# The modulation product of block 1's mixers: fp32 weights against split halves with four stationary columns

## The chip, the cores and the metric

The kernel runs on one core of a Trainium2 chip. The metric is device time in microseconds (us) of one execution. The median of three executions of the kernel before is 5227.35 us (5226.25 to 5237.21). The engines are named as in the profile: PE is the matrix engine (PEld its weight loads), DVE the vector engine, ACT the scalar engine, SP the engine that issues the transfers of the weights.

## The reference, cut to what matters

The model is two blocks. Block 1 has attention beside a state-space mixer and a feed-forward layer. Block 2 is modulated: two conditioning vectors of 2048 numbers go through SiLU and one matrix, and the six parts of the result shift, scale and gate the block's activations.

```python
# block 2, one layer; c_ctx serves the context, c the tokens
mod_c = jax.nn.silu(c_ctx) @ w_ada[l][:, :n_mod * D_MODEL] + b_ada[l][:n_mod * D_MODEL]
mod   = jax.nn.silu(c)     @ w_ada[l] + b_ada[l]          # 2048 -> 6 * 2048
sh1, sc1, g1, sh2, sc2, g2 = [m[:, None, :] for m in jnp.split(mod, 6, axis=-1)]
y, _ = _token_mixers(_modulate(x, sh1, sc1), lp, ctx_states, True, True)
```

`w_ada` is 2048 x 12288 in fp32, 100 MB. Nothing in it depends on block 1, so the kernel computes the product while block 1's mixers run.

## The kernel before, in words

All weights stream through one ring of 8 slots of 128x512 fp32 (`weights_ring`). SP issues the transfer of a chunk (256 KB) when the chunk 8 places ahead of it is marked `ring_free`. A group is 512 output columns. A group of `w_ada` is 16 chunks, one per 128 of the 2048 inputs, and there are 24 groups, so 384 chunks.

Most products are split (`split_scalar`, `split_vector`, `split_tensor`): for every chunk ACT copies the weights into the type fp32r (`weights_hi`, L511), DVE subtracts that from the chunk (`weights_lo`, L526), and PE multiplies low weights by high activations, high by low and high by high (L547 to L549). There are 5 pairs of halves in rotation. `w_ada` is not split before the change: `modulation_tensor` multiplies the fp32 chunk as the moving operand (512 columns) against two stationary columns, the two vectors (`cc`, L1088). That takes nothing from ACT or DVE but, once a group, ACT's copy of the 2x512 result (L1101) and its store.

The stage around the change is `mixers1`. It has 4 turns. In a turn, two strands run in lockstep: attention (8 units of a head and a query tile, 6 pieces each) and two channel blocks of the state-space mixer (16 pieces each). `beside` gives, after every piece of the strands, as many steps of the background as keep pace with 56 pieces; the background is six groups of `w_ada` of 17 steps, of which 16 are chunks. So each piece is followed by 102/56 = 1.82 steps, that is 1.71 chunks, and the strands end after 49 pieces; the steps left over run by themselves at the turn's end. The three engines write out their instructions in this same order, each for its own part. The order of an engine is the order of its code, and one semaphore counts each engine's finished instructions, so nothing is reordered at run time.

The pieces of a channel block, by number, on DVE: 1 masks and copies (L1025, L1026, L625); 2 the phases (L1034); 3 L1037; 4 L1040, then ACT's sine (L1073), L1042, then ACT's cosine (L1075); 5 empty; 6 to 13 the eight inner steps j; 14 L1057; 15 L1059; 16 L1061; and L1065 at the start of the next block, behind PE's sixteen products L1013 and L1014. An inner step is: PE multiplies twice (L1006, L1007), DVE forms the rotated input (L1049, L1050, L1052) and scans it (L1054). PE's next pair waits for L1050 (`turned`). A unit of attention is PE L863, DVE L892, L895, L897, ACT L923 and L924 (exponential), DVE L900, L902, L904, PE L870, DVE L908 and L909, PE L876, DVE L625.

Of the kernel before, what the change touches and what calls it, by code (L numbers as in the profile page):

```python
# [6 lines left out]
F32 = mybir.dt.float32  # L7
# [237 lines left out]
class Kernel:  # L245
# [4 lines left out]
    def __init__(self, nc, io, known, pofs, cofs):  # L250
        self.nc, self.io, self.pofs, self.cofs = nc, io, pofs, cofs
        self.s = Signals(nc, known)
        self.s.sem("vector_done")
        sb = lambda name, *shape, dt=F32: nc.alloc_sbuf_tensor(name, [P, *shape], dt)
        self.ring = sb("weights_ring", self.SLOTS, self.COLS)
        self.whi, self.wlo = (sb(n, self.HALVES, self.COLS, dt=F32R) for n in ("weights_hi", "weights_lo"))
        self.acc = [nc.alloc_psum_tensor(f"acc{m}", [P, 512], F32) for m in range(4)]
        self.bank = [nc.alloc_psum_tensor(f"bank{b}", [P, 512], F32) for b in range(4)]
        self.params = sb("params_sb", max(b for a, b in pofs.values()))
        self.consts = sb("consts_sb", max(b for a, b in cofs.values()))  # L260
        self.res = sb("residual", KD, L)

        with nc.sbuf_tensor("moving_halves", [P, KD, 512], F32R) as self.xin_r:
            pass
        self.xin = sb("moving", KD, 512)
        self.mix = sb("mixed", 16, T)
        self.rstd = sb("rstd", L)
        self.mods = sb("mods", 96, 2)
        self.cc, self.cc_sig = sb("cc", 32), sb("cc_sig", 32)
        self.mods_row = sb("mods_row", 512)  # L270
        self.ab = sb("ab", 4, 32)
        self.whole = sb("whole_i32", 64, dt=I32)[:, :]
        with nc.sbuf_tensor("arena_halves", [P, ARENA], F32R) as self.arena_r:
# [97 lines left out]
    def plan(self):  # L371
# [30 lines left out]
        for n in range(5):  # L402
            add("w_in", n, io["w_in"], n, KD, L, keep_projection, **x1)
        for n in range(24):
            add("w_ada", n, io["w_ada"], n, KD, 0, None)
        for n in range(2):
            add("w_glu", n, io["w_glu"], n, 8, T, keep_gate, **moving(T))
        for n in range(4):
# [24 lines left out]
        for g in order:  # L433
            g.ring0, g.split0 = ring, split
            ring += g.kchunks
            split += g.kchunks if g.split else 0
            side = g.index % 2 if g.split else 0
            banks = [0] if g.name == "w_ada" else range(4 * side, 4 * side + 4) if g.tokens > T else range(2 * side, 2 * side + 2)
            if g.name == "read" and g.split:
                banks = [0, 1] if side else [4, 5]  # L440
            at = [(self.acc + self.bank)[b] for b in banks]
            if g.name == "w_ada":
                g.out = [at[0][0:2, :]]
            elif g.tokens > T:
                g.out = [at[m][:, 0:g.tokens] for m in range(4)]
            else:
                g.out = [at[m // 2][:, T * (m % 2):T * (m % 2 + 1)] for m in range(4)]
            g.shared = 0 < g.tokens <= T
            g.before = sorted({holder[b] for b in banks if b in holder})
            for b in banks:  # L450
                holder[b] = (g.name, g.index)
# [316 lines left out]
def project1_scalar(k):  # L768
# [3 lines left out]
    a.dma_start(k.res[:, :, :], io["hT"].rearrange("(c p) t -> p c t", p=P)).then_inc(*s.landed("inputs", "inputs"))  # L772
    a.wait_ge(*s.at("inputs"))
    a.activation(k.cc_sig[:, :], k.p("c"), ACT.Sigmoid).then_inc(*s.made("scalar_done", "cc_sig"))
    squares_scalar(k, "rms1", k.res[:, :, :], k.squares1, L)
    split_scalar(k, k.some("w_in", *range(5)), {0: operand_scalar("w_in", lambda kc: k.squares1[:, kc, :])})
    barrier(k, "scalar", "project1")
# [7 lines left out]
def project1_vector(k):  # L785
    v, s = k.nc.vector, k.s
    v.wait_ge(*s.at("inputs"))
    v.wait_ge(*s.at("cc_sig"))
    v.tensor_tensor(k.cc[:, :], k.p("c"), k.cc_sig[:, :], ALU.mult).then_inc(*s.made("vector_done", "cc"))
    root_vector(k, "rms1", KD, L)  # L790
    make = lambda k, c: normalise(k, k.res[:, :, :], k.p("norm_mix_g"), k.squares1, c, L)
    split_vector(k, k.some("w_in", *range(5)), {0: operand_vector("w_in", lambda kc: k.squares1[:, kc, :], make)})
    barrier(k, "vector", "project1")
# [285 lines left out]


def modulation_tensor(k, g):
    pe, s = k.nc.tensor, k.s
    ccv = k.cc[:, :].rearrange("p (c m) -> p c m", m=2)
    for name, index in g.before:
        pe.wait_ge(*s.at("drained", name, index))
    for kc in range(g.kchunks):
        pe.wait_ge(*s.at("weights", g.ring0 + kc))
        mm = pe.matmul(g.out[0], ccv[:, kc, :], k.slot(g.ring0 + kc), start=kc == 0, stop=kc == g.kchunks - 1)  # L1088
        mm.then_inc(*s.made("tensor_done", "ring_free", g.ring0 + kc))
        yield  # L1090
    s.mark("tensor_done", "summed", g.name, g.index)
    yield

def modulation_scalar(k, g):
    a, s = k.nc.scalar, k.s
    for _ in range(17):
        yield
    a.wait_ge(*s.at("summed", g.name, g.index))
    if g.index:
        a.wait_ge(*s.at("mods_out", g.index - 1))  # L1100
    a.activation(k.mods_row[0:2, :], g.out[0], ACT.Copy).then_inc(*s.made("scalar_done", "drained", g.name, g.index))  # L1101
    a.wait_ge(*s.now("scalar_done"))
    a.dma_start(k.io["s_mods"][:, 512 * g.index:512 * g.index + 512], k.mods_row[0:2, :]).then_inc(
        *s.landed("mods_out", "mods_out", g.index))

def modulation_vector(k, g):
    for _ in range(17):
        yield

def pair_of(channels, k, turn):  # L1110
    yield from channels(k, 2 * turn)
# [7 lines left out]
def mixers1_tensor(k):  # L1119
    heads_tensor(k)  # L1120
    barrier(k, "tensor", "heads")
    k.nc.tensor.wait_ge(*k.s.at("cc"))
    mixers1(k, attention_tensor, channels_tensor, modulation_tensor)
    barrier(k, "tensor", "mixers1")

# [16 lines left out]
def output1_scalar(k):  # L1142
# [13 lines left out]
    split_scalar(k, k.feed_forward("w_up", "w_down"), {0: operand_scalar("w_up", lambda kc: k.mix[:, kc, :])})  # L1156
    barrier(k, "scalar", "w_down")
    a.wait_ge(*s.at("mods_out", 23))
    rows = k.mix[0:96, 0:2, 0:P]
    for r in range(2):  # L1160
        a.dma_start(rows[:, r, :], k.io["s_mods"][r:r + 1, :].rearrange("a (c p) -> (a c) p", p=P)).then_inc(*s.landed("mods_in"))
    s.mark("mods_in", "mods_in")

def output1_tensor(k):
# [7 lines left out]
    squares_tensor(k, "rms2", k.mix, KD, T)  # L1172
    split_tensor(k, k.feed_forward("w_up", "w_down"))
    barrier(k, "tensor", "w_down")
    rows = k.mix[0:96, 0:2, 0:P]
    pe.wait_ge(*s.at("mods_in"))
    for r in range(2):
        pe.transpose(k.bank[r][:, 0:96], rows[:, r, :], k.ident[0:96, 0:96]).then_inc(*s.made("tensor_done", "mods_t", r))

def output1_vector(k):  # L1180
# [23 lines left out]
    for r in range(2):  # L1204
        v.wait_ge(*s.at("mods_t", r))
        serial(k, v.tensor_tensor(k.mods[:, :, r], k.bank[r][:, 0:96], k.p("b_ada"), ALU.add))
    for c in (16, 64):
        serial(k, v.tensor_scalar(k.mods[:, c:c + 16, :], k.mods[:, c:c + 16, :], 1.0, None, ALU.add, ALU.bypass))

# [1072 lines left out]
```

## Time and profile before

| | us |
|---|---|
| median of three executions | 5227.35 |
| the profiled execution | 5236.34 |
| its span, first to last instruction | 5234.9 |
| PE busy in the span | 4389.1 |
| DVE busy | 2903.7 |
| ACT busy | 1562.3 |

Busy time says how long an engine had something running; a wait inside a stage shows in the views of that stage. The program runs stage by stage with barriers between. The stage of the mixers lies between about 195 us, where PE's first product of the modulation starts, and 870 us. Times in the rows below are us from the start of the span unless they are marked ns. "x4" after a row is the count of records in it. A product of fp32 by fp32 is recorded twice, so the 384 products of L1088 are 768 records.

### The profile page before, as it was taken

What the parts mean: (1) busy time and instruction counts of PE and PEld (TensorE: products, weight loads), DVE (VectorE), ACT (ScalarE), POOL (GpSimd) and SP (SyncE); (2) the same over time, 40 slices, a digit from 0 to 9 for tenths busy, and PEclk for the clock granted to TensorE, in tenths of its full rate; (3) what the DMA queues carried; (4) which work ended last, traced back from release to release, by engine and by line L of the source; (5) the groups of instructions that cost most, each with busy time, mean ns of one, the idle gap of its engine ahead of it and who ended that gap; (6) DMA issues with size and microseconds to landing.
All of it is one profiled execution on the core that took longest, in us unless ns stands there. A gap on an engine that the chain in (4) does not pass through costs nothing.

```text
span 5234.9 us, 70641 instructions
## 1 busy us (share of the span) xinstructions
PE 4389.1 (84%) x28352; PEld 3731.8 (71%) x28352; DVE 2903.7 (55%) x6102; ACT 1562.3 (30%) x2706; POOL 0.2 (0%) x4
## 2 busy tenths in 40 slices
PE   7588887899999899993478876788775798999997
PEld 7323323799999888892467766677662397999997
DVE  4745544575565522345665666656626475755654
ACT  4211111454444322342122121221200043544442
POOL 0000000000000000000000000000000000000000
PEclk9799998999999999995689988899896799999999
DMA  5354454465656544571222222222240163555553
GB/s 176 97 171 141 141 163 147 129 186 185 184 186 183 158 121 122 144 198 45 60 69 81 61 64 71 68 83 61 62 129 22 39 208 128 178 189 184 184 185 113
DMA packets 383061, 669.57 MB, mean 128 GB/s; under 512 B 43897, under 2 KB 77402, under 8 KB 382220
## 3 DMA queue, kind: packets, MB, share of 16 engines
q1 hardware_dynamic: 327168, 595.74, 38.0%
q10 hardware_dynamic: 55564, 69.31, 4.0%
q8 instruction: 223, 3.65, 0.3%
q14 instruction: 106, 0.87, 0.1%
HBM read 634.87 MB, written 29.46 MB: 127 GB/s over the span
## 4 chain that ended last, share of the span: by engine, by line
PE 64%; DVE 13%; ACT 2%; issue 2%; DMA 1%; ACTq 1%; DVEq 0%
PE acc L547 13%; PE acc L549 12%; PE acc L548 12%; PE acc L589 8%; PE bank L1611 2%; PE bank L547 2%; PE bank L549 2%; PE bank L548 2%; PE bank L1620 2%; PE bank L1618 1%; PE bank L2005 1%; DVE arena L1466 1%; DMA arena<-s_read 1%; ACT weights_hi L511 1%; PE acc L1435 1%
## 5 line engine op out<-in xcount | busy, mean ns | idle before, releaser
L526 DVE TENSOR_TENSOR weights_lo<-weights_ring,weights_hi 128x512 fp32r<-128x512 f32 x1600 | 1093.9, 691 | 1042.5 <-ACT weights_hi L511 1041.1
L511 ACT ACTIVATE weights_hi<-weights_ring 128x512 fp32r<-128x512 f32 x1600 | 992.9, 629 | 1102.6 <-PE acc L549 905.3
L548 PE MATMUL acc<-arena_halves,weights_hi 128*128 128x256 f32 (+2 forms) x3136 | 925.3, 295 | 0.0
L547 PE MATMUL acc<-arena_halves,weights_lo 128*128 128x256 f32 (+1 forms) x2944 | 870.0, 296 | 18.2 <-DVE weights_lo L526 17.9
L549 PE MATMUL acc<-arena_halves,weights_hi 128*128 128x256 f32 (+1 forms) x2944 | 869.1, 295 | 0.0
L547 PE MATMUL acc<-moving_halves,weights_lo 128*128 128x256 f32 (+1 forms) x2816 | 795.7, 283 | 69.8 <-DVE weights_lo L526 68.3
L549 PE MATMUL acc<-moving_halves,weights_hi 128*128 128x256 f32 (+1 forms) x2816 | 791.0, 281 | 0.0
L548 PE MATMUL acc<-moving_halves,weights_hi 128*128 128x256 f32 x2624 | 735.8, 280 | 0.0
L548 PEld LDWEIGHTS acc<-arena_halves,weights_hi 128*128 128x128 f32 x3136 | 602.4, 192 | 12.6
L547 PEld LDWEIGHTS acc<-moving_halves,weights_lo 128*128 128x128 f32 x2816 | 538.6, 191 | 77.7 <-DVE weights_lo L526 50.5
L547 PEld LDWEIGHTS acc<-arena_halves,weights_lo 128*128 128x128 f32 x2944 | 565.7, 192 | 31.9 <-DVE weights_lo L526 12.3
L549 PEld LDWEIGHTS acc<-arena_halves,weights_hi 128*128 128x128 f32 x2944 | 565.7, 192 | 12.9
L589 PE MATMUL acc<-moving,weights_ring 128*128 128x256 f32 x2304 | 554.3, 387 | 2.1 <-ACT arena L692 2.1
L549 PEld LDWEIGHTS acc<-moving_halves,weights_hi 128*128 128x128 f32 x2816 | 535.1, 190 | 0.0
L548 PEld LDWEIGHTS acc<-moving_halves,weights_hi 128*128 128x128 f32 x2624 | 499.7, 190 | 0.0
L589 PEld LDWEIGHTS acc<-moving,weights_ring 128*128 128x128 f32 x2304 | 428.8, 195 | 52.3 <-ACT arena L692 2.5
L1088 PE MATMUL acc<-weights_ring,cc 128*2 128x512 f32 x768 | 367.0, 614 | 12.2 <-ACT mods_row L1101 12.1
L1088 PEld LDWEIGHTS acc<-weights_ring,cc 128*2 128x2 f32 x768 | 55.2, 85 | 244.7 <-issue 219.0
L548 PE MATMUL bank<-arena_halves,weights_hi 128*128 128x256 f32 (+2 forms) x640 | 209.0, 327 | 0.0
L549 PE MATMUL bank<-arena_halves,weights_hi 128*128 128x512 f32 (+1 forms) x512 | 172.0, 336 | 0.0
L547 PE MATMUL bank<-arena_halves,weights_lo 128*128 128x512 f32 (+1 forms) x512 | 172.0, 336 | 0.0
L1739 ACT ACTIVATE arena<-bank 128x512 f32<-128x512 f32 x112 | 65.7, 594 | 298.7 <-PE bank L1611 297.1
(409 smaller groups left out, 5088.8 us busy)
## 6 DMA issues: line engine op xcount, KB each, us to landing
weights_ring<-in_w_in SPq DMA_DIRECT2D x624, 256.0 KB, 2.7
weights_ring<-in_w_ff SPq DMA_DIRECT2D x512, 256.0 KB, 3.0
weights_ring<-in_w_ada SPq DMA_DIRECT2D x384, 256.0 KB, 3.0
weights_ring<-in_w_up SPq DMA_DIRECT2D x256, 256.0 KB, 3.0
weights_ring<-in_w_down SPq DMA_DIRECT2D x256, 256.0 KB, 3.3
weights_ring<-in_w_out SPq DMA_DIRECT2D x128, 256.0 KB, 3.2
weights_ring<-in_w_branch SPq DMA_DIRECT2D x96, 256.0 KB, 3.2
s_state<-arena ACTq DMA_DIRECT2D x36, 256.0 KB, 2.9
```

Source lines behind the costliest of these rows:

```text
L511: a.activation(whi, k.slot(g.ring0 + kc), ACT.Copy).then_inc(*s.made("scalar_done", "high", n))
L526: v.tensor_tensor(wlo, k.slot(g.ring0 + kc), whi.bitcast(F32), ALU.subtract).then_inc(*s.made("vector_done", "low", n))
L547: pe.matmul(g.out[m], wlo[:, cols], xhi, start=first, stop=False, skip_group_check=g.shared)
L548: pe.matmul(g.out[m], whi[:, cols], xlo, start=False, stop=False, skip_group_check=g.shared)
L549: mm = pe.matmul(g.out[m], whi[:, cols], xhi, start=False, stop=last, skip_group_check=g.shared)
L589: mm = pe.matmul(g.out[m], k.slot(g.ring0 + kc)[:, m * P:(m + 1) * P], g.x(kc), start=kc == 0 and m % 2 == 0, stop=last, skip_group_check= ...
L1088: mm = pe.matmul(g.out[0], ccv[:, kc, :], k.slot(g.ring0 + kc), start=kc == 0, stop=kc == g.kchunks - 1)
L1435: mm = pe.matmul(po[:, P * j:P * j + P], h["lev"][:, j, :], h["lev"][:, j, :], start=True, stop=True)
L1466: own(v.reciprocal(f, f))
L1611: mm = pe.matmul(b0[:, P * j:P * j + P], mt[:, j, :], x[:, j, :], start=True, stop=True)
L1620: mm = pe.matmul(b1[:, P * j:P * j + P], y[:, j, :], xt[:, j, :], start=True, stop=True)
L1739: a.activation(d["y"], tiles(b0), ACT.Copy).then_inc(*s.made("scalar_done", *ev("kept", level)))
```

## The change

The modulation is split as the other products are. In `modulation_scalar` ACT makes the high half of each chunk; in `modulation_vector` DVE makes the low half and thereby marks the ring slot free; in `modulation_tensor` PE multiplies each half, 128x512 as the moving operand, against four stationary columns (`cc_halves`): the high halves of both vectors and their low halves. The four rows of the result are stored instead of two, read back by four transfers, transposed, and added in pairs.

```diff
+        self.cc4 = sb("cc_halves", KD, 4, dt=F32R)
...
-            add("w_ada", n, io["w_ada"], n, KD, 0, None)
+            add("w_ada", n, io["w_ada"], n, KD, 0, None, high=lambda kc: self.cc4[:, kc, :])
...
-                g.out = [at[0][0:2, :]]
+                g.out = [at[0][0:4, :]]
...
     a.activation(k.cc_sig[:, :], k.p("c"), ACT.Sigmoid).then_inc(*s.made("scalar_done", "cc_sig"))
+    a.wait_ge(*s.at("cc"))
+    a.activation(k.cc4[:, :, 0:2], k.cc[:, :].rearrange("p (c m) -> p c m", m=2), ACT.Copy).then_inc(*s.made("scalar_done", "cc_high"))
...
+    v.wait_ge(*s.at("cc_high"))
+    v.tensor_tensor(k.cc4[:, :, 2:4], ccv, k.cc4[:, :, 0:2].bitcast(F32), ALU.subtract).then_inc(*s.made("vector_done", "cc4"))
...
 def modulation_tensor(k, g):
     for kc in range(g.kchunks):
-        pe.wait_ge(*s.at("weights", g.ring0 + kc))
-        mm = pe.matmul(g.out[0], ccv[:, kc, :], k.slot(g.ring0 + kc), start=kc == 0, stop=kc == g.kchunks - 1)
-        mm.then_inc(*s.made("tensor_done", "ring_free", g.ring0 + kc))
+        n, whi, wlo = halves(k, g, kc)
+        pe.wait_ge(*s.at("low", n))
+        pe.matmul(g.out[0], k.cc4[:, kc, :], wlo, start=kc == 0, stop=False)
+        pe.matmul(g.out[0], k.cc4[:, kc, :], whi, start=False, stop=kc == g.kchunks - 1).then_inc(
+            *s.made("tensor_done", "halves_used", n))
         yield
...
 def modulation_scalar(k, g):
     a, s = k.nc.scalar, k.s
-    for _ in range(17):
-        yield
+    for kc in range(g.kchunks):
+        n, whi, wlo = halves(k, g, kc)
+        a.wait_ge(*s.at("weights", g.ring0 + kc))
+        a.wait_ge(*s.at("halves_used", n - k.HALVES))
+        a.activation(whi, k.slot(g.ring0 + kc), ACT.Copy).then_inc(*s.made("scalar_done", "high", n))
+        yield
+    yield
     a.wait_ge(*s.at("summed", g.name, g.index))
...
 def modulation_vector(k, g):
-    for _ in range(17):
-        yield
+    v, s = k.nc.vector, k.s
+    for kc in range(g.kchunks):
+        n, whi, wlo = halves(k, g, kc)
+        v.wait_ge(*s.at("high", n))
+        v.tensor_tensor(wlo, k.slot(g.ring0 + kc), whi.bitcast(F32), ALU.subtract).then_inc(*s.made("vector_done", "low", n))
+        s.mark("vector_done", "ring_free", g.ring0 + kc)
+        yield
+    yield
...
-    for r in range(2):
+    for r in range(4):
         a.dma_start(rows[:, r, :], k.io["s_mods"][r:r + 1, :].rearrange("a (c p) -> (a c) p", p=P)).then_inc(*s.landed("mods_in"))
...
+    for r in range(2):
+        v.wait_ge(*s.at("mods_t", r + 2))
+        serial(k, v.tensor_tensor(k.mods[:, :, r], k.mods[:, :, r], k.bank[r + 2][:, 0:96], ALU.add))
```

The lines move by a few numbers: L1006 before is L1012 after, L1049 is L1055, L1054 is L1060.

On DVE, among the inner steps of the first channel block, before the change the end of one step is followed by the start of the next, with attention's small instructions between:

```order
L1049 TENSOR_TENSOR arena<-arena,acc 128x272 [waits tensor_done]
L1050 TENSOR_TENSOR rstd<-arena,acc 128x272
L1052 TENSOR_TENSOR arena<-arena,rstd 128x272 [waits vector_done]
L1054 SCALAR_TENSOR_TENSOR arena<-arena 128x272 [waits vector_done]
L895 TENSOR_REDUCE moving<-moving 128x1 [waits vector_done]
L897 TENSOR_SCALAR moving<-moving,params_sb 128x1 [waits vector_done]
```

After it, at the same place, one or two subtractions stand behind each step's scan:

```order
L1055 TENSOR_TENSOR arena<-arena,acc 128x272 [waits tensor_done]
L1056 TENSOR_TENSOR rstd<-arena,acc 128x272
L1058 TENSOR_TENSOR arena<-arena,rstd 128x272 [waits vector_done]
L1060 SCALAR_TENSOR_TENSOR arena<-arena 128x272 [waits vector_done]
L1124 TENSOR_TENSOR weights_lo<-weights_ring,weights_hi 128x512 [waits scalar_done] x2
L901 TENSOR_REDUCE moving<-moving 128x1 [waits vector_done]
L903 TENSOR_SCALAR moving<-moving,params_sb 128x1 [waits vector_done]
```

Nothing on DVE changes its place; the subtractions stand between what stood side by side.

On PE at the same place, before the change, the modulation's products stand between two inner steps and wait for a transfer (`arrived`) alone:

```order
L1006 MATMUL acc<-arena 128x272 [waits vector_done]
L1007 MATMUL acc<-arena 128x272
L1088 MATMUL acc<-weights_ring,cc 2x512 [waits arrived3]
L1088 MATMUL acc<-weights_ring,cc 2x512 [waits arrived4]
L1006 MATMUL acc<-arena 128x272 [waits vector_done]
L1007 MATMUL acc<-arena 128x272
```

After it they stand at the same places, two for one, and the first of each two waits for DVE (`vector_done`):

```order
L1012 MATMUL acc<-arena 128x272 [waits vector_done]
L1013 MATMUL acc<-arena 128x272
L1095 MATMUL acc<-weights_lo,cc_halves 4x512 [waits vector_done]
L1096 MATMUL acc<-weights_hi,cc_halves 4x512
L1095 MATMUL acc<-weights_lo,cc_halves 4x512 [waits vector_done]
L1096 MATMUL acc<-weights_hi,cc_halves 4x512
L1012 MATMUL acc<-arena 128x272 [waits vector_done]
L1013 MATMUL acc<-arena 128x272
```

The next inner step's L1012 stands behind products that wait for DVE, as it stood behind products that waited for a transfer.

On ACT, in the first channel block, the sine and cosine stood before the change like this:

```order
L1073 ACTIVATE arena<-arena 128x2176 [waits vector_done]
L1075 ACTIVATE arena<-arena,consts_sb 128x2176 [waits vector_done]
L923 ACT_TABLE_LOAD
L923 ACTIVATE moving<-moving 128x272 [waits vector_done]
```

After it, high halves stand before and behind them:

```order
L1108 ACTIVATE weights_hi<-weights_ring 128x512 [waits tensor_done,arrived5]
L1079 ACT_TABLE_LOAD
L1079 ACTIVATE arena<-arena 128x2176 [waits vector_done]
L1081 ACTIVATE arena<-arena,consts_sb 128x2176 [waits vector_done]
L1108 ACTIVATE weights_hi<-weights_ring 128x512 [waits tensor_done,arrived6]
```

The chunks of piece 4 get their high halves behind the cosine.

## Rows read from the trace of the kernel before

**Rows 1.** Stretches: PE, PEld, DVE, ACT, POOL busy (count); granted clock, DMA share, GB/s.

```profile
195.00:870.00 675.00, 575.50 (x1638) 199.44 (x1638) 359.05 (x779) 98.90 (x158) 0.00 (x0) 0.93 0.49 153
454.00:478.00 24.00, 23.12 (x73) 8.61 (x73) 18.60 (x44) 1.44 (x5) 0.00 (x0) 0.99 0.45 133
3920.00:4000.00 80.00, 35.02 (x71) 13.84 (x72) 57.13 (x122) 2.12 (x3) 0.00 (x0) 0.50 0.15 42
4012.00:4046.00 34.00, 18.01 (x42) 6.58 (x40) 22.34 (x19) 0.00 (x0) 0.00 (x0) 0.84 0.00 0
```

**Rows 2.** Groups by line, 195 to 870 us.

```profile
L1088 PE MATMUL acc<-weights_ring,cc 128*2 128x512 f32 x768 | 367.0, 614 | 12.2 <-ACT mods_row L1101 12.1
```

**Rows 3.** Timeline of DVE: blocks, inner steps, a unit of attention, turns.

```profile
435.21 0.42 DVE L1065 TENSOR_TENSOR mixed<-arena,acc 128x256 f32<-128x256 f32 x1 [6.97 <-PE acc L1014]
448.18 2.42 DVE L1042 SCALAR_TENSOR_TENSOR arena<-arena 128x2176 f32<-128x2176 f32 x1 [2.08 <-ACT arena L1073]
454.15 0.44 DVE L1049 TENSOR_TENSOR arena<-arena,acc 128x272 f32<-128x272 f32 x1 [2.88 <-PE acc L1007]
...
466.77 0.44 DVE L1049 TENSOR_TENSOR arena<-arena,acc 128x272 f32<-128x272 f32 x1 [0.33 <-PE acc L1007]
...
468.71 0.13 DVE L900 TENSOR_TENSOR moving<-moving 128x1 f32<-128x1 f32 x1
...
478.04 2.41 DVE L1057 TENSOR_TENSOR arena<-arena 128x2176 f32<-128x2176 f32 x1
490.95 0.42 DVE L1065 TENSOR_TENSOR mixed<-arena,acc 128x256 f32<-128x256 f32 x1 [5.55 <-PE acc L1014]
...
501.07 0.50 DVE L892 SCALAR_TENSOR_TENSOR moving<-consts_sb,bank 128x272 f32<-128x272 f32 x1 [2.18 <-PE bank L863]
513.95 0.50 DVE L892 SCALAR_TENSOR_TENSOR moving<-consts_sb,bank 128x272 f32<-128x272 f32 x1 [2.17 <-PE bank L863]
```

**Rows 4.** Timeline of PE: an inner step, attention's products, the chain of sixteen.

```profile
465.55 0.73 PE L1006 MATMUL acc<-arena 128*128 128x272 f32 x2
466.67 1.88 PE L1088 MATMUL acc<-weights_ring,cc 128*2 128x512 f32 x4
468.48 0.72 PE L1006 MATMUL acc<-arena 128*128 128x272 f32 x2
...
483.24 0.72 PE L1013 MATMUL acc<-arena 128*128 128x272 f32 x2 [1.18 <-DVE arena L1059]
...
510.32 1.12 PE L876 MATMUL bank<-moving 128*128 128x128 f32 x6
513.18 0.72 PE L863 MATMUL bank<-moving,arena 64*128 64x272 f32 x2
...
523.26 7.03 PE L1088 MATMUL acc<-weights_ring,cc 128*2 128x512 f32 x16
```

**Rows 5.** Timeline of PE and DVE, an inner step at the lower clock.

```profile
554.27 1.27 PE L1006 MATMUL acc<-arena 128*128 128x272 f32 x2
556.56 0.44 DVE L1049 TENSOR_TENSOR arena<-arena,acc 128x272 f32<-128x272 f32 x1 [1.90 <-PE acc L1007]
```

**Rows 6.** Timeline of PE, two fp32r products of 512 columns.

```profile
2000.19 0.39 PE L547 MATMUL acc<-arena_halves,weights_lo 128*128 128x512 f32 x1
2000.42 0.39 PE L548 MATMUL acc<-arena_halves,weights_hi 128*128 128x512 f32 x1
```

**Rows 7.** Timeline of DVE and PE: a low half, what follows it.

```profile
891.17 0.69 DVE L526 TENSOR_TENSOR weights_lo<-weights_ring,weights_hi 128x512 fp32r<-128x512 f32 x1
891.78 0.42 DVE L574 TENSOR_TENSOR moving_halves<-arena,moving_halves 128x256 fp32r<-128x256 f32 x1
892.01 0.55 PE L547 MATMUL acc<-moving_halves,weights_lo 128*128 128x256 f32 x1 [19.52 <-DVE weights_lo L526]
```

**Rows 8.** The page, the groups of the low and the high halves.

```profile
L526 DVE TENSOR_TENSOR weights_lo<-weights_ring,weights_hi 128x512 fp32r<-128x512 f32 x1600 | 1093.9, 691 | 1042.5 <-ACT weights_hi L511 1041.1
L511 ACT ACTIVATE weights_hi<-weights_ring 128x512 fp32r<-128x512 f32 x1600 | 992.9, 629 | 1102.6 <-PE acc L549 905.3
```

More of the change, by code:

```diff
@@ L789, in project1_vector @@
     v.tensor_tensor(k.cc[:, :], k.p("c"), k.cc_sig[:, :], ALU.mult).then_inc(*s.made("vector_done", "cc"))
+    ccv = k.cc[:, :].rearrange("p (c m) -> p c m", m=2)
+    v.wait_ge(*s.at("cc_high"))
+    v.tensor_tensor(k.cc4[:, :, 2:4], ccv, k.cc4[:, :, 0:2].bitcast(F32), ALU.subtract).then_inc(*s.made("vector_done", "cc4"))
     root_vector(k, "rms1", KD, L)
@@ L1082, in modulation_tensor @@
     pe, s = k.nc.tensor, k.s
-    ccv = k.cc[:, :].rearrange("p (c m) -> p c m", m=2)
     for name, index in g.before:
@@ L1100, in modulation_scalar @@
         a.wait_ge(*s.at("mods_out", g.index - 1))
-    a.activation(k.mods_row[0:2, :], g.out[0], ACT.Copy).then_inc(*s.made("scalar_done", "drained", g.name, g.index))
+    a.activation(k.mods_row[0:4, :], g.out[0], ACT.Copy).then_inc(*s.made("scalar_done", "drained", g.name, g.index))
     a.wait_ge(*s.now("scalar_done"))
-    a.dma_start(k.io["s_mods"][:, 512 * g.index:512 * g.index + 512], k.mods_row[0:2, :]).then_inc(
+    a.dma_start(k.io["s_mods"][:, 512 * g.index:512 * g.index + 512], k.mods_row[0:4, :]).then_inc(
         *s.landed("mods_out", "mods_out", g.index))
 def modulation_vector(k, g):
-    for _ in range(17):
+    v, s = k.nc.vector, k.s
[4 more added lines that the diff above has]
+        s.mark("vector_done", "ring_free", g.ring0 + kc)
         yield
+    yield
 def pair_of(channels, k, turn):
@@ L1121, in mixers1_tensor @@
     barrier(k, "tensor", "heads")
-    k.nc.tensor.wait_ge(*k.s.at("cc"))
+    k.nc.tensor.wait_ge(*k.s.at("cc4"))
     mixers1(k, attention_tensor, channels_tensor, modulation_tensor)
@@ L1158, in output1_scalar @@
     a.wait_ge(*s.at("mods_out", 23))
-    rows = k.mix[0:96, 0:2, 0:P]
-    for r in range(2):
+    rows = k.mix[0:96, 0:4, 0:P]
+    for r in range(4):
         a.dma_start(rows[:, r, :], k.io["s_mods"][r:r + 1, :].rearrange("a (c p) -> (a c) p", p=P)).then_inc(*s.landed("mods_in"))
@@ L1174, in output1_tensor @@
     barrier(k, "tensor", "w_down")
-    rows = k.mix[0:96, 0:2, 0:P]
+    rows = k.mix[0:96, 0:4, 0:P]
     pe.wait_ge(*s.at("mods_in"))
-    for r in range(2):
+    for r in range(4):
         pe.transpose(k.bank[r][:, 0:96], rows[:, r, :], k.ident[0:96, 0:96]).then_inc(*s.made("tensor_done", "mods_t", r))
@@ L2267 @@
     scratch = {"s_state": (4608, 2 * T), "s_read": (6656, T), "s_gate": (6144, T),
-               "s_mods": (2, 6 * DM), "s_kf": (512, 512), "s_qf": (512, T), "s_kt": (512, 512), "s_vt": (1024, 512)}
+               "s_mods": (4, 6 * DM), "s_kf": (512, 512), "s_qf": (512, T), "s_kt": (512, 512), "s_vt": (1024, 512)}
     def built(known):
```

## The prediction

> **What bounds the kernel now.** I read the busy time by stretch first. In the stage of the mixers, 195 to 870 us, PE is busy 575.5 of 675 us, DVE 359.05 and ACT 98.9, at a granted clock of 0.93 [rows 1]. The reader is to see that PE looks like the bound and that DVE has 316 us to spare. The groups by line say what fills PE: L1088 has 367.0 us in 768 records [rows 2]. Then the timelines, since a spare engine means little where engines hand work to each other. On DVE the wait at L1065 lasts 6.97 and 5.55 us and at L1049 between 0.33 and 2.88 us [rows 3]: DVE waits for PE and not the other way round. On PE the modulation's products fill the time between one inner step's pair and the next [rows 4]: L1006 at 465.55, L1088 from 466.67 on, L1006 again at 468.48. While DVE does its 1.9 us of the step, PE does two chunks. PE needs DVE only for L1006, which is ready when PE comes to it. That is the cover that the change touches.
>
> **What goes from PE.** Eight chunks (16 records) begin at 523.26 and take 7.03 us until their last end [rows 4], so a chunk costs about 0.86 us. Afterwards it is two fp32r products of 512 columns; two such start 0.23 us apart [rows 6], so 0.45 us a chunk. 384 x 0.41 = 157 us of PE's time go, and PE has about 418 us of work left in the stage.
>
> The Trainium skill, TensorE: Matmul & The Clock Gate, section "Architectural detail", says that PE's queue can pull weight loads ahead of products in flight, while DVE and ACT are strictly in order. By that rule the load of the next L1012 would be done while PE waits for a low half, an estimate of 0.2 us a step or 13 us over 64 (the pair takes 1.22 us until L1049, and its two products, at the chain of sixteen's 7.7 us for 16, 0.96). The rows do not show it for a load that itself waits for DVE, and I leave it out of the sum.
>
> **What comes to ACT and DVE.** A high half takes ACT 629 ns, a low half DVE 691 ns [rows 8]. An instruction behind a low half starts 0.61 us after it (891.17 and 891.78) [rows 7], so I take 0.60 us a chunk: DVE gets 384 x 0.60 = 230 us and then has 589 us of work in the stage. ACT gets 242 us and has 341. Neither alone exceeds 675 us. What decides is the handing over.
>
> **The inner steps.** There are 64 (8 blocks of 8). Before, the eight of the second block of a turn lie between 454.15 and 478.04 [rows 3], 2.99 us each. After the change the order of the engines closes a loop. PE may start the pair of step j+1 only behind the modulation's products of piece j, these wait for DVE's low halves, and DVE makes those only behind its work on step j. Once round: DVE from L1049 to the end of the scan 1.94 us (466.77 to 468.71) [rows 3], then 1.71 low halves at 0.60, 1.03, and 0.09 until the last one's real end (0.69 against 0.60). From that end to PE's start 0.15 us (891.86 to 892.01) [rows 7]. The last chunk's two products 0.45. Attention's products before the pair, 0.35 on average: three pieces of six have them, the dearest L876 with 1.12 us and L863 with 0.72 [rows 4]; I take about 0.5 for L870, and records overlap a little. The pair until DVE's L1049, 1.22 us (465.55 to 466.77) [rows 3, 4]. The sum is 5.23 us; DVE's own small attention work lies beside PE's. So 64 x (5.23 - 2.99) = 143 us more.
>
> **The pieces around them.** From L1065 at 435.21 to the first L1049 at 454.15 are 18.94 us, of which DVE waits 2.08 for the sine, 0.5 elsewhere and 2.88 at L1049 [rows 3]. After: 13.5 of own work, 8.5 low halves 5.1, the sine 2.1, then the low halves of piece 4, whose high halves stand behind the cosine on ACT (as long as the sine, 2.1, and 0.63), 2.7; two of attention's handovers from PE (0.15 + 0.45 + about 0.95 each), 3.1; the loop's 0.15 + 0.45 + 1.22. That is 28.3, 9.4 more. From L1057 at 478.04 to L1065 at 490.95 are 12.9 us [rows 3]. After: two passes over 2176 columns 4.7, 3.4 low halves 2.05, attention 1.1 and a handover 1.35, 0.6 to PE, and the chain of sixteen from 483.24 to 490.95, 7.7 [rows 3, 4]. That is 17.5, 4.6 more. Together 14 us a block, 112 us for 8. Here before the wait of 5.55 to 6.97 us was no spare time: the chain of sixteen is what it waited for.
>
> **Attention alone.** A unit takes 12.88 us before (501.07 to 513.95) [rows 3], with some 11 chunks on PE. After: DVE 2.8 of attention and 10.3 low halves, 6.2; three handovers 4.2; the low halves behind L897 wait for ACT's exponential and a high half, about 1.6; part of a group's end, where ACT copies the result before the next high half, 0.6. 15.4 us, 2.5 more, for 2.8 units in each of 4 turns: 29 us. The rest of a turn's tail runs at 0.86 us a chunk on PE before and 0.6 plus two ends of groups (1.8 each) after, which comes out even.
>
> **Ends.** ACT's copy of the vectors stands before its first squares and waits for DVE: 0.5 to 1 us. Two more transfers, transposes and additions at the end of block 1: 1 to 3 us. 3 us together. Transfers of weights are not nearer: the ring moves 153 GB/s here and the stage gets longer.
>
> Sum at the same clock: 143 + 112 + 29 + 3 = 287 us.
>
> **The clock.** The engine falls to 1.2 GHz in stretches. PE had 85% of the stage busy and a granted clock of 0.93, so some 14% of it low. After, about 418 us of PE's work lie in about 960 us, 44%. Two stretches are near that: 3920 to 4000 us, busy 35.0 of 80, at 0.50; 4012 to 4046, busy 18.0 of 34, at 0.84 [rows 1]. Busy time is itself longer at the low clock, so the second is nearer; I take 0.80, 40% low. The price: at the low clock an inner pair takes 2.29 us until L1049 (554.27 to 556.56) [rows 5] against 1.22, the last chunk 0.45 more, attention about 0.3 more, 1.8 a step, 115 us; the chain of sixteen doubles, 7 us for each of 8, 57; the 64 other handovers 0.9 each, 57. 229 us if all were low, and (0.40 - 0.14) x 229 = 60 us for my share. Its ends are 0 (clock unchanged) and 197 (all low).
>
> The sum is 287 + 60 = 347. The profiled execution took 5236.34 us, 9 over the median, so it would become 5583 and the median 5574.
>
> **Rivals.** First, faster: DVE and ACT run ahead and PE was the bound, so the stage falls to DVE's work, 589 us, 86 less, about 5141. For it speak 316 idle us on DVE. Against it speaks the order: a low half can't be ahead of the step before it in DVE's code, and L1012 not ahead of the product that waits for it. It decides for this case if the wait at L1055 after the change stays below about 0.4 us.
>
> Second, the loop closes but its price is half, since the waits I add in a row overlap (low halves made while PE does attention's products, high halves up to five ahead): 287 becomes about 140, clock 30, 5400.
>
> Third, the clock stays low nearly all the stage: 287 + 197, 5711. For it speaks the stretch at 0.50 with DVE the busier engine; against it 0.84 at 53%.
>
> Fourth, the change does not do what it says, PE's time per chunk stays at 0.86 us. Rows 6 show fp32r with 128 stationary columns and not 4. It would add 0.41 a step where the loop closes and 0.41 a handover, about 55 us: 5630.
>
> **How the numbers follow.** Forecast 0.58, the half price 0.16, the clock low nearly all 0.12, the fourth 0.04, faster 0.07, and within 0.2% (10 us, about what a measurement of this kernel can tell from no change) 0.03. The range 5410 to 5740 leaves out the faster and the unchanged cases and the outer parts of the others. Slower takes all but 0.10.
>
> **What would show it.** Right: the stage ends near 1200 us on the trace; inner steps 5 to 6 us apart; DVE's wait at L1055 around 1.8 us for PE at every step; PE's L1095 waits for DVE's L1124 some hundred times; PE's busy time in the stage falls by over 100 us (less the low clock's part) and no stage after it changes. Wrong: L1055 waits little and steps stay near 3 us; or L1095 waits for transfers; or the steps are 5 us apart but PE's products wait for ACT's high halves instead, which would be a bound by ACT that I hold for piece 4 alone.

## The result and the profile after

The changed kernel takes 5582.57 us (median of 4, 5579.51 to 5586.22), the kernel before 5228.04 us. The ratio is 1.0675 with a 95% interval of 1.0656 to 1.0693: slower by 354 us, where 5574 us and a range of 5410 to 5740 were forecast.

The page after, busy time over the span. PE's busy time did not fall [before: 4389.1, 2903.7 and 1562.3 us]:

```profile
PE 4390.3 (79%) x28354; PEld 3782.9 (68%) x28354; DVE 3139.8 (56%) x6489; ACT 1778.7 (32%) x3091; POOL 0.2 (0%) x4
```

The busy time by stretch after: the stage of the mixers up to its end, and the first seven intervals between inner steps of the third channel block (columns as in rows 1; the last three numbers are the granted clock, the DMA share and GB/s).

```profile
195.00:1219.00 1024.00, 582.63 (x1632) 257.93 (x1632) 596.75 (x1170) 311.47 (x541) 0.00 (x0) 0.64 0.32 101
497.00:544.00 47.00, 27.88 (x65) 13.07 (x63) 23.16 (x50) 6.91 (x14) 0.00 (x0) 0.59 0.20 62
```

The stage ends where ACT squares the attention result. That was at 865 us and is at 1219 us, so it took 670 us and takes 1024. The whole difference is here. The granted clock went from 0.93 [rows 1] to 0.64. PE's busy time in the stage is 583 us and was 573, although its work is less: with the same new products and nobody to wait for, PE is busy 432 us (the run "products alone" below). At the lower clock a product lasts longer, and a product that starts after a wait does not overlap the one before it (at the high clock one is recorded with 0.40 us, and two start 0.23 us apart). DVE has 238 us of work more and 427 us of idle time where it had 311, and 238 + 116 are the 354 us. ACT has 216 us of work more. (The two profiled executions differ by 347.5 us as a whole, since that of the kernel before was 9 us over its median.)

The groups of the new lines by line, 195 to 1222 us:

```profile
L1124 DVE TENSOR_TENSOR weights_lo<-weights_ring,weights_hi 128x512 fp32r<-128x512 f32 x384 | 246.1, 682 | 53.4 <-ACT weights_hi L1108 52.8
L1108 ACT ACTIVATE weights_hi<-weights_ring 128x512 fp32r<-128x512 f32 x384 | 218.7, 620 | 128.7 <-PE acc L1096 112.9 <-ACT mods_row L1114 6.7 <-DMA weights_ring<-in_w_ada 5.4
L1096 PE MATMUL acc<-weights_hi,cc_halves 128*4 128x512 f32 x384 | 205.9, 536 | 0.0
L1095 PE MATMUL acc<-weights_lo,cc_halves 128*4 128x512 f32 x384 | 203.6, 530 | 434.3 <-DVE weights_lo L1124 433.8
```

And the waits of the stage, longest in total first (engine and line that waited, what for: us in total, times, longest):

```profile
PE acc L1095 <- DVE weights_lo L1124: 433.8, 161, 30.8
...
DVE arena L1055 <- PE acc L1013: 135.6, 64, 3.8
```

PE stood 433.8 us before L1095 for DVE's low halves (30.8 of them at the stage's start), and DVE 135.6 us at all 64 inner steps for PE: 2.1 us each time. Two engines that wait for each other in turn are a closed loop. Before, PE waited for no low half, and DVE's wait at the same line was 0.8 us in the mean of 64 steps:

```profile
DVE arena L1049 <- PE acc L1007: 53.1, 60, 2.9
```

One turn of the loop in the timeline, DVE and PE after. This answers to the inner step of [rows 3, 4].

```profile
510.77 0.44 DVE L1055 TENSOR_TENSOR arena<-arena,acc 128x272 f32<-128x272 f32 x1 [2.58 <-PE acc L1013]
512.06 0.72 DVE L1060 TENSOR_TENSOR_SCAN arena<-arena 128x272 f32<-128x272 f32 x1
512.71 1.27 DVE L1124 TENSOR_TENSOR weights_lo<-weights_ring,weights_hi 128x512 fp32r<-128x512 f32 x2
516.72 0.44 DVE L1055 TENSOR_TENSOR arena<-arena,acc 128x272 f32<-128x272 f32 x1 [2.08 <-PE acc L1013]
...
513.42 0.59 PE L1095 MATMUL acc<-weights_lo,cc_halves 128*4 128x512 f32 x1 [2.69 <-DVE weights_lo L1124]
514.66 0.63 PE L1096 MATMUL acc<-weights_hi,cc_halves 128*4 128x512 f32 x1
515.09 1.11 PE L1012 MATMUL acc<-arena 128*128 128x272 f32 x2
```

DVE ends its two low halves at 513.98. PE has the second chunk's products behind it, then the pair L1012 and L1013 at the low clock, and DVE goes on at 516.72: 5.95 us for a step. PE's load of the weights of L1012, which the prediction considered and left out of its sum, did not run ahead of the wait in this step: it starts at 514.67, when PE's wait has been over for 1.25 us.

```profile
514.67 0.33 PEld L1012 LDWEIGHTS acc<-arena 128*128 128x128 f32 x1 [0.30 <-DVE moving L910]
```

From DVE's timeline, the means over the eight channel blocks of one execution of each kernel: a block's start to its first inner step 18.6 us before and 29.2 after; the seven intervals between inner steps 3.19 and 6.32 each; from the last inner step to L1065 (after: L1071) 15.6 and 25.0; attention alone with the rest of the turn 47.0 and 50.9. That is 8 x (10.6 + 7 x 3.13 + 9.3) + 4 x 3.9 = 350 us.

### The profile page after: what moved, and what is told of

Its sections match the earlier page's. It is cut to its first block, busy times and chain, and to the rows that moved or that the text cites. A ratio compares the mean times of both kernels' runs of the same rounds, so it can differ in the third digit from the quotient of the medians.

```text
span 5582.4 us, 71805 instructions
## 1 busy us (share of the span) xinstructions
PE 4390.3 (79%) x28354; PEld 3782.9 (68%) x28354; DVE 3139.8 (56%) x6489; ACT 1778.7 (32%) x3091; POOL 0.2 (0%) x4
## 4 chain that ended last, share of the span: by engine, by line
PE 58%; DVE 13%; ACT 2%; issue 2%; DMA 1%; ACTq 1%; DVEq 0%
PE acc L548 11%; PE acc L550 11%; PE acc L549 11%; PE acc L590 8%; PE bank L1633 2%; PE bank L550 2%; PE bank L549 2%; PE bank L548 2%; PE bank L1642 2%; PE bank L1640 1%; PE bank L2027 1%; DMA arena<-s_read 1%; ACT weights_hi L512 1%; DVE arena L1488 1%; PE acc L1457 1%
## 5 line engine op out<-in xcount | busy, mean ns | idle before, releaser
L527 DVE TENSOR_TENSOR weights_lo<-weights_ring,weights_hi 128x512 fp32r<-128x512 f32 x1600 | 1094.2, 691 | 1034.7 <-ACT weights_hi L512 1033.2
L512 ACT ACTIVATE weights_hi<-weights_ring 128x512 fp32r<-128x512 f32 x1600 | 993.2, 629 | 1096.3 <-PE acc L550 898.0
L548 PEld LDWEIGHTS acc<-arena_halves,weights_lo 128*128 128x128 f32 x2944 | 565.5, 192 | 31.1 <-DVE weights_lo L527 11.6
L1095 PE MATMUL acc<-weights_lo,cc_halves 128*4 128x512 f32 x384 | 203.6, 530 | 434.3 <-DVE weights_lo L1124 433.8
L1095 PEld LDWEIGHTS acc<-weights_lo,cc_halves 128*4 128x4 f32 x384 | 32.3, 84 | 632.0 <-DVE weights_lo L1124 545.7
L1124 DVE TENSOR_TENSOR weights_lo<-weights_ring,weights_hi 128x512 fp32r<-128x512 f32 x384 | 246.1, 682 | 53.4 <-ACT weights_hi L1108 52.8
L1108 ACT ACTIVATE weights_hi<-weights_ring 128x512 fp32r<-128x512 f32 x384 | 218.7, 620 | 128.7 <-PE acc L1096 112.9
L1096 PE MATMUL acc<-weights_hi,cc_halves 128*4 128x512 f32 x384 | 205.9, 536 | 0.0
```

Source lines behind the costliest of these rows:

```text
L512: a.activation(whi, k.slot(g.ring0 + kc), ACT.Copy).then_inc(*s.made("scalar_done", "high", n))
L527: v.tensor_tensor(wlo, k.slot(g.ring0 + kc), whi.bitcast(F32), ALU.subtract).then_inc(*s.made("vector_done", "low", n))
L548: pe.matmul(g.out[m], wlo[:, cols], xhi, start=first, stop=False, skip_group_check=g.shared)
L1095: pe.matmul(g.out[0], k.cc4[:, kc, :], wlo, start=kc == 0, stop=False)
L1096: pe.matmul(g.out[0], k.cc4[:, kc, :], whi, start=False, stop=kc == g.kchunks - 1).then_inc(*s.made("tensor_done", "halves_used", n))
L1108: a.activation(whi, k.slot(g.ring0 + kc), ACT.Copy).then_inc(*s.made("scalar_done", "high", n))
```

## The experiments

Each ran beside the kernel before on one chip; the row of the change is the result above. The kernel before took 5232.4 us beside the first four, 5226.8 beside "later, with filler" and the two with POOL, and 5227.5 beside the last three; differences from it in the text are against these. The stage's end, its granted clock and an inner step's mean are from one profiled execution of each.

| kernel | median us | ratio to before, 95% interval | stage ends | clock | inner step |
|---|---|---|---|---|---|
| before | 5228 | 1 | 865 | 0.93 | 3.19 |
| the change | 5582.6 | 1.0656 to 1.0693 | 1219 | 0.64 | 6.32 |
| halves made, unread | 5339.1 | 1.0186 to 1.022 | 973 | 0.89 | 3.38 |
| products alone | 5152.6 | 0.983 to 0.986 | 783 | 0.86 | 2.58 |
| PE two chunks later | 5311.5 | 1.0133 to 1.0163 | 942 | 0.78 | 3.32 |
| filler on PE | 5494.3 | 1.0487 to 1.0519 | 1129 | 0.77 | 4.92 |
| later, with filler | 5319.5 | 1.0159 to 1.019 | 958 | 0.83 | 3.62 |
| low halves on POOL | 5438.7 | 1.0388 to 1.0419 | 1074 | 0.73 | 3.72 |
| POOL, and later | 5379.3 | 1.0274 to 1.0308 | 1014 | 0.78 | 3.51 |
| last 2 groups of 6 | 5226.6 | 0.9987 to 1.0005 | 862 | 0.90 | 3.27 |
| last 3 groups of 6 | 5225.6 | 0.9987 to 1.0005 | 858 | 0.88 | 3.22 |
| last group of 6 | 5225.7 | 0.9985 to 1.0003 | 861 | 0.92 | 3.17 |

**Halves made, unread.** ACT and DVE do all the new work in the new places; PE multiplies as before.

```diff
-        pe.wait_ge(*s.at("low", n))
-        pe.matmul(g.out[0], k.cc4[:, kc, :], wlo, ...)
-        pe.matmul(g.out[0], k.cc4[:, kc, :], whi, ...).then_inc(*s.made("tensor_done", "halves_used", n))
+        pe.wait_ge(*s.at("weights", g.ring0 + kc))
+        mm = pe.matmul(g.out[0], ccv[:, kc, :], k.slot(g.ring0 + kc), ...)
+        mm.then_inc(*s.made("tensor_done", "ring_read", g.ring0 + kc))
...
+        s.mark("vector_done", "halves_used", n)     # in modulation_vector
+                sp.wait_ge(*s.at("ring_read", n - k.SLOTS))     # in weights_sync
```

> ACT and DVE make all 768 halves of the modulation's weights at the same places as after the change, but nothing reads them: PE multiplies the fp32 chunk by two columns as before the change and waits for transfers alone. My theory (the price is PE's products waiting behind DVE in the order, and the low clock that follows): DVE has 597 us of work in the stage, an inner step costs 3.0 to 3.5 us, the stage is 680 to 760 us and the kernel 5240 to 5320 us, with a granted clock in the stage over 0.85. Rival (the 246 us of low halves and 219 us of high halves are themselves the price): 5470 us or more.

5339 us, 107 over before and 243 under the change. The stage is 778 us, inner steps 3.38 us and the clock 0.89. The theory's direction is right and its upper bound was 19 us too low; the rival (5470 or more) falls. The new work of ACT and DVE costs about 107 us even where nobody waits for its result. It lies in the pieces around the inner steps: the start of a block takes 25.6 us against 18.6, its end 20.1 against 15.6. PE still has its 157 us of fp32 work in this version, so the 107 us are the price beside the old products, and not a term that can be added to the next run's.

**Products alone.** The other half of the change by itself. PE reads halves that are left over from an earlier product, so this kernel leaves out the modulation's values; it shows times alone.

```diff
     for kc in range(g.kchunks):
-        n, whi, wlo = halves(k, g, kc)
-        pe.wait_ge(*s.at("low", n))
-        pe.matmul(g.out[0], k.cc4[:, kc, :], wlo, ...)
-        pe.matmul(g.out[0], k.cc4[:, kc, :], whi, ...)
+        pe.wait_ge(*s.at("weights", g.ring0 + kc))
+        pe.matmul(g.out[0], k.cc4[:, kc, :], k.wlo[:, kc % 5, :], ...)
+        pe.matmul(g.out[0], k.cc4[:, kc, :], k.whi[:, kc % 5, :], ...)
```

> PE makes the two fp32r products per chunk with four columns, but from halves left over from an earlier product, so the modulation's values are not computed; ACT and DVE make no halves, PE waits for transfers alone. Theory: PE loses 157 us of work and waits for nobody new, so the stage gets shorter by 60 to 120 us at the same clock and loses part of that to a lower clock: 5120 to 5200 us. Rival (a product with four stationary columns is slow, or the low clock by itself costs 135 us or more): 5230 us or more.

5153 us, 80 faster than before, as the theory had it. About half of the 157 us that PE loses come back as time, 56 of them where attention runs alone (32.9 us a turn against 47.0), so PE bound a good part of the stage before, though not all of it; the clock fell from 0.93 to 0.86. Products with four stationary columns are as cheap as those with 128 [rows 6], 0.23 us from start to start:

```profile
502.04 0.40 PE L1093 MATMUL acc<-weights_lo,cc_halves 128*4 128x512 f32 x1
502.27 0.40 PE L1094 MATMUL acc<-weights_hi,cc_halves 128*4 128x512 f32 x1
502.51 0.39 PE L1093 MATMUL acc<-weights_lo,cc_halves 128*4 128x512 f32 x1
```

So the change has a gain of 80 us in it and loses it, with 354 more, elsewhere.

**PE two chunks later.** All the work of the change, in another order on PE and for ACT's copy of a group's result.

```diff
+LAG = 2
 def modulation_tensor(k, g):
+    if g.index % 6 == 0:
+        for _ in range(LAG):
+            yield
...
         a.activation(whi, k.slot(g.ring0 + kc), ACT.Copy).then_inc(*s.made("scalar_done", "high", n))
+        if kc == LAG and g.index:
+            modulation_out(k, k.groups["w_ada", g.index - 1])
         yield
```

> The changed kernel with PE's products of the modulation two chunks later in PE's order than the halves are in DVE's (and ACT's copy of a group's result three chunks into the next group). Theory: the loop is open, an inner step falls from 6.2 us to 3.5 (high clock) or 4.5 (low clock), and attention's handovers get shorter: 5330 to 5450 us. Rival (work of ACT and DVE as such): within 20 us of 5583.

5311 us, 271 less than the change by the order alone (PE's products and ACT's copy of the result moved together; the share of each was not measured) and 19 better than the theory's best case. The busy time of the stage:

```profile
195.00:942.00 747.00, 483.04 (x1632) 215.44 (x1631) 587.27 (x1167) 308.46 (x541) 0.00 (x0) 0.78 0.43 138
```

DVE has about the work of the change (587 us, and 597 there) and takes 747 us for the stage and not 1024. In DVE's timeline an inner step such as this one has no wait left (all 64 together have 17.8 us, where the change had 135.6):

```profile
507.42 0.43 DVE L1055 TENSOR_TENSOR arena<-arena,acc 128x272 f32<-128x272 f32 x1
508.70 0.72 DVE L1060 TENSOR_TENSOR_SCAN arena<-arena 128x272 f32<-128x272 f32 x1
509.35 1.27 DVE L1134 TENSOR_TENSOR weights_lo<-weights_ring,weights_hi 128x512 fp32r<-128x512 f32 x2
...
511.13 0.43 DVE L1055 TENSOR_TENSOR arena<-arena,acc 128x272 f32<-128x272 f32 x1
```

This is the experiment that shows the cause: the same instructions, other neighbours. 3.71 us a step with two low halves, and no releaser behind L1055. What remains against before is 79 us. DVE has 228 us more work than before and 151 us less idle time (160 us against 311), and the added time lies where it does in the version that only makes the halves: the start of a block takes 26.0 us against 18.6, its end 19.7 against 15.6. PE still waits 150 us for low halves and 84 us for ACT's copies of results, ACT 116 us for PE. How much of the 79 us is DVE's work as such, and how much these waits, was not tried; a lag other than two chunks was not run either.

**Filler on PE.** Does the low clock cost anything in the closed loop?

```diff
         pe.matmul(pair[1][:, 0:L], k.lb2[:, j, :], k.t_u, ...).then_inc(*s.made("tensor_done", "driven", c, j))
+        for _ in range(3):
+            pe.matmul(k.acc[1][0:2, 0:256], k.cc[:, 0:2], k.consts[:, 0:256], start=True, stop=True)
```

> The changed kernel with three idle fp32 products of 256 columns behind each of the 64 inner pairs on PE, into a bank that nobody reads, in the 2.7 us in which PE waits for the low halves there. Theory: the granted clock in the stage rises from 0.64 to 0.80 or more and gives back 50 to 120 us: 5460 to 5530 us. Rival (the clock has little part, or filler comes in the way): 5583 or up to 60 us above it.

5494 us, 88 less than the change, with 192 products more. The stage and a stretch of inner steps:

```profile
195.00:1129.00 934.00, 583.10 (x2016) 240.80 (x2016) 594.78 (x1168) 311.71 (x541) 0.00 (x0) 0.77 0.35 110
483.00:519.00 36.00, 24.86 (x102) 9.91 (x101) 25.75 (x52) 8.75 (x20) 0.00 (x0) 1.00 0.28 88
```

The clock in the stage was forecast at 0.80 or more and was 0.77, since the filler stands at inner steps only; there it is 1.00. The theory's time is met. Two steps of its DVE timeline at the full clock, and the same place on PE:

```profile
487.99 0.44 DVE L1057 TENSOR_TENSOR arena<-arena,acc 128x272 f32<-128x272 f32 x1 [1.04 <-PE acc L1013]
492.82 0.44 DVE L1057 TENSOR_TENSOR arena<-arena,acc 128x272 f32<-128x272 f32 x1 [0.96 <-PE acc L1013]
...
490.64 0.39 PE L1097 MATMUL acc<-weights_lo,cc_halves 128*4 128x512 f32 x1 [1.31 <-DVE weights_lo L1126]
```

The mean of the 49 intervals that lie wholly in the high clock is 4.87 us. In the changed kernel, 22 intervals lie wholly in the low clock, with a mean of 6.37 us. These are not all the same places in a block; the 19 intervals that are wholly low in the change and wholly high here take 6.33 and 4.69 us. So the clock is worth about 1.6 us a step, and the loop at the high clock costs 4.87 where before it was 3.0 (47 intervals). The one interval of the change that lies wholly in the high clock agrees: 4.84 us, and 4.85 at the same place here. PE's wait for the low half, in the steps shown, is 1.31 us behind the filler against 2.69 without: the filler used PE's idle time.

**Later, with filler.**

> PE's products two chunks later and three idle products behind each inner pair. Theory: with the loop open PE's idle time in a step is about 1 us instead of 2.7, so the filler of 1.3 us (2.6 at the low clock) comes in the way while the clock rises: within 40 us of 5311, and above 0.85 granted in the stage. Rival (the low clock costs here what it cost in the closed loop): 5220 to 5260 us.

Its edit is the two above together. 5319.5 us, 8 over the version without filler (14 if each is set against its own kernel before), as the theory says; the stage's clock was forecast over 0.85 and was 0.83. Inner steps were already at the high clock in the open loop (52 of 56 intervals), so the filler had nothing to win there; they got 0.3 us longer. At the inner steps, then, the low clock came with the closed loop and went with it, and inside the loop it had a price, the 88 us above.

**Low halves on POOL.** If DVE's order is the trouble, another engine with no order to keep could make them.

```diff
+def modulation_pool(k, g):
+    p, s = k.nc.gpsimd, k.s
+    for kc in range(g.kchunks):
+        n, whi, wlo = halves(k, g, kc)
+        p.wait_ge(*s.at("high", n))
+        p.tensor_tensor(wlo, k.slot(g.ring0 + kc), whi.bitcast(F32), ALU.subtract).then_inc(*s.made("pool_done", "low", n))
+        s.mark("pool_done", "ring_free", g.ring0 + kc)
```

> The changed kernel with the low halves made by POOL, which does nothing else here, instead of DVE; the order on PE, ACT and DVE is otherwise that of the change. Theory (the loop through DVE's order is the price): the loop is open but for ACT's high halves, DVE has 359 us of work again, and the stage falls from 1024 us to 620 to 720: 5170 to 5280 us. Rival (a split through any other engine costs the handing over anyway, or POOL's subtraction is too slow or slows DVE): 5350 us or more. POOL's time for 128x512 is not in any trace so far; between 0.7 us (DVE's) and 1.7 us it is hidden, since 384 of them have 650 us.

5439 us. The theory's forecast (5170 to 5280) fails, by more than 150 us, and the rival's second half is right. DVE's busy time in the stage was forecast back at 359 us and is 451. POOL's group, and four of DVE's, 195 to 1000 us:

```profile
L1128 POOL TENSOR_TENSOR weights_lo<-weights_ring,weights_hi 128x512 fp32r<-128x512 f32 x341 | 470.0, 1411 | 532.4 <-ACT weights_hi L1108 532.4
L1060 DVE TENSOR_TENSOR_SCAN arena<-arena 128x272 f32<-128x272 f32 x64 | 62.6, 979 | 2.2
L1058 DVE TENSOR_TENSOR arena<-arena,rstd 128x272 f32<-128x272 f32 x64 | 43.0, 672 | 2.2
L1056 DVE TENSOR_TENSOR rstd<-arena,acc 128x272 f32<-128x272 f32 x64 | 27.4, 429 | 0.0
L910 DVE TENSOR_SCALAR moving<-moving 128x272 f32<-128x272 f32 x29 | 22.9, 791 | 1.0
```

A low half takes POOL 1.41 us in the mean. I had called that hidden, since 384 of them fit into 650 us. They fit in sum and not where they are needed: in the tail of a turn PE took a chunk every 0.86 us before, POOL needs 1.28 us for one in the median, and attention alone took 57.7 us a turn against 47.0. And POOL slows DVE: the scan from 724 to 979 ns, L1058 from 442 to 672, while L1056, which reads PSUM, stays at 429. The Trainium skill, SBUF — State Buffer, section "Who interferes with whom", says that a DVE instruction with two inputs in SBUF contends with a POOL instruction that reads SBUF, and that the ports they share are an exclusive lock. The trace agrees for these three: the two with both inputs in SBUF wait, the one with an input in PSUM does not, and the wait is all or nothing (half of the 64 scans take 725 ns or less, a quarter 1670 or more). But two inputs are not the whole of it here: L910, which has one input tile, in SBUF, goes from 362 ns in the change to 791.

**POOL, and two chunks later.**

> Low halves by POOL and PE's modulation products two chunks later, both. Theory: as the version that only multiplies (5153 us) plus what is left of waits for ACT: 5150 to 5230 us, faster than the kernel before. Rival as for the one with POOL alone: no better than that one, 5350 or more.

Both edits. 5379 us. The theory's 5150 to 5230 fails; the rival's 5350 or more holds, but not its "no better than that one": the kernel is 59 us better than with POOL alone, so a hand-over through ACT's and POOL's place in the order also had a price, and 68 worse than DVE with the same lag. The scan is at 1217 ns. POOL's group to 1000 us, and DVE's scan:

```profile
L1138 POOL TENSOR_TENSOR weights_lo<-weights_ring,weights_hi 128x512 fp32r<-128x512 f32 x374 | 503.2, 1379 | 496.6 <-ACT weights_hi L1113 496.6
L1060 DVE TENSOR_TENSOR_SCAN arena<-arena 128x272 f32<-128x272 f32 x64 | 77.9, 1217 | 2.2
```

**Split only where attention is alone.** There DVE has little to do. Groups with these numbers in a turn are split, with the lag; the others are one fp32 product against the same four columns.

```diff
+LAG, SPLIT = 2, (4, 5)        # (3, 4, 5) and (5,) in the others
...
+        if g.split:
+            pe.wait_ge(*s.at("low", n))
...
+        else:
+            pe.matmul(g.out[0], k.cc4[:, kc, :].bitcast(F32), k.slot(g.ring0 + kc), ...)
```

> Only the last two of a turn's six groups are split, in the stretch where attention runs alone and DVE has 15% to do; PE takes them two chunks later. The first four stay fp32 products, against the same four columns. Theory (the price was the handing over beside the inner steps, and PE is the bound where attention is alone): the inner steps keep their 3 us, a unit of attention falls from 12.9 to about 10 us and a chunk of the tail from 0.86 to about 0.62: 25 to 45 us less than before, 5180 to 5205 us. Rival (the low clock and the waits at a group's end take it back): 5220 to 5240 us.

> The last three of six groups split; the third from the end lies beside the last inner steps of the second channel block. Theory: within 15 us of the one with two groups, since what is won at the pieces behind the inner steps is lost at the two or three steps that it meets: 5170 to 5215 us. Rival as there: 5230 us or more.

> Only the last group of six split, in the tail, where nothing runs beside it for most of its chunks. Theory: about 13 chunks a turn at 0.2 us less and a third of a unit of attention, less the wait for the last two chunks at a turn's end: 8 to 18 us less than before, 5210 to 5220 us. Rival: no difference.

All three are the same as before within the measurement: 0.9996 (0.9987 to 1.0005), 0.9996 (0.9987 to 1.0005), 0.9994 (0.9985 to 1.0003), each the ratio of 11 executions to 27. The forecast gains (8 us at the least, 57 at the most) did not come. With two groups, attention alone takes 44.5 us a turn against 47.0. With three it takes 40.4, but the end of each turn's second channel block takes 19.8 us against 15.6. The stage ends 3 and 7 us earlier than before, and the median is 1 and 2 us lower (the profiled execution of the version with three was 5.5 us under its median, so its 7 us are more than is typical). In the timeline of the version with three, DVE has waits for ACT and for PE where low halves stand behind the exponential:

```profile
512.24 0.50 DVE L898 SCALAR_TENSOR_TENSOR moving<-consts_sb,bank 128x272 f32<-128x272 f32 x1
515.92 1.29 DVE L1142 TENSOR_TENSOR weights_lo<-weights_ring,weights_hi 128x512 fp32r<-128x512 f32 x2 [1.38 <-ACT weights_hi L1128]
522.25 0.29 DVE L626 TENSOR_SCALAR moving<-bank 64x128 f32<-64x128 f32 x1 [1.45 <-PE bank L882]
```

A unit of attention takes 11.6 us there (L898 at 500.67 and at 512.24) and not the 10 expected. No version with the whole computation beat the kernel before by more than the measurement can tell.

## Why the prediction was right, and where it was not

**The mechanism** was right and is shown. PE's products stand behind DVE's low halves, and the next inner step stands behind PE's products. Opening the loop, with every instruction kept, gives back 271 of 354 us. The first rival (faster, 5141 us) fell: DVE waits 2.1 us at L1055 where that rival needed under 0.4. Of the signs, PE waited for L1124 at L1095 161 times and the stage ended at 1219 us, as said; the steps were a little longer (6.32 us for 5 to 6).

**What goes from PE** was right in its size: PE's part alone is worth 80 us less, of 157 us less work. The fourth rival falls with it: with four columns too there are 0.23 us between starts at the high clock. The sign that PE's busy time in the stage would fall by over 100 us did not come: it rose by 10, and shows the 141 us less only in the version with the products alone (432 us against 573).

**The inner steps.** The sum had 5.23 us at the high clock; the measured mean is 4.87. The excess over 3.0 is 1.87 and not 2.24, so the term of 143 us should have been 120. Part of it is the count: two blocks have 22 low halves in their 14 intervals, 1.57 each and not 1.71.

**The pieces around them** were forecast at 14 us a block at the same clock, and attention's unit at 15.4. A unit measured from L898 to L898:

```profile
677.40 0.50 DVE L898 SCALAR_TENSOR_TENSOR moving<-consts_sb,bank 128x272 f32<-128x272 f32 x1 [1.38 <-PE bank L869]
692.97 0.50 DVE L898 SCALAR_TENSOR_TENSOR moving<-consts_sb,bank 128x272 f32<-128x272 f32 x1 [1.37 <-PE bank L869]
```

That is 15.57 us, at a granted clock of 0.78. But attention alone grew by only 3.9 us a turn, 16 us in all for a term of 29. The pieces around the inner steps came to 19.9 us a block, clock included (10.6 + 9.3, of which one inner step's excess of 3.1 is in the second), so about 16.8 for them. Of this the forecast had 14 and part of the clock's term. How much of the rest is the clock's was not measured apart.

**The clock** was the term that was mis-sized most. I took 0.80 from two stretches of a like busy share and it was 0.64: the low clock held 72% of the stage and not 40%. By my own price of 229 us for all of it, the term would have been (0.72 - 0.14) x 229 = 133 us and not 60. The price was also somewhat high: a step costs about 1.6 us more at the low clock and not 1.8. With 133 in the place of 60, the terms at the same clock leave about 354 - 133 = 221 for what I put at 287. So the agreement of the whole to 9 us (5574 against 5583) is luck: two errors of opposite sign met, 73 us too little for the clock and some 66 too much for the rest. This split is worked out with the prediction's own price and was not measured.

**The ends** were put at 3 us. At the start ACT's first squares begin at 20.39 against 19.76 us, 0.6 later; between the reading of the modulation's rows and the first instruction behind it (L1213, after: L1235) the distance is 0.6 us longer (the first instruction waits in both for a transfer of weights that is issued behind the reads, now two reads later). 1.2 us together.

**The second rival**, half the price because waits overlap, fell in the time (5400), but its reason has something in it: the 221 us that are left for the terms at the same clock lie about halfway between the forecast's 287 and its 140. The third, the low clock nearly all the stage (5711), fell too: with 72% the clock came out about midway between the forecast's 40% and all.

## What to carry to other kernels

Where several engines work off one interleaved order, an operation that is made to wait for another engine's piece of the same position closes a loop through everything behind it on both. Sum the loop (one engine's whole piece, the hand-over, the other's whole piece) and compare it with the period before, since neither engine's busy time shows it: DVE had 316 us to spare and the stage got 354 us longer. The first cure to try is to let the consumer run a piece or two later than the producer, and before that to ask whether the producer's work fits into the stage at all: here even the open loop stayed 79 us behind.

## What the runs showed of the hardware that was not expected

- The low clock fed on the loop: in a stretch of inner steps of 6.7 us, where no wait of PE was over 2.8 us, the granted clock was 0.59. With three idle products a step (1.46 us on the timeline) it was 1.00 there, and the kernel was 88 us faster.
- A subtraction of 128x512 from SBUF takes POOL 1.28 us in the median and 1.38 to 1.40 in the mean against DVE's 0.68. In the two kernels that use POOL for it, DVE's scan over 272 columns goes from 0.72 us to 0.98 and 1.22 in the mean, with 1.70 at the worst.
- An fp32r product with 4 stationary columns costs what one with 128 does, 0.23 us for 512 moving columns.
